# The first mixers' loop: sigmoids written as tanh, and inverse roots as a power on GpSimd ahead of the gate's product

## The chip, the cores and the metric

One core of one Trainium2 chip runs one program. The metric is the device time of one execution in microseconds, the median of several runs, together with one profiled execution whose trace is read below.

## The reference

The program computes two model blocks in a row. The change is in the first block, in the part that the reference calls `retention` and `rwkv7_time_mix`. Cut to what matters:

```python
w = -softplus(-(w0 + tanh(w_lo) @ w_up)) - 0.5
decay = exp(-exp(w))                       # = exp(-exp(-0.5) * sigmoid(...))
a = sigmoid(a0 + a_lo @ a_up)
g = sigmoid(g_lo) @ g_up
kk = k * k_k;  kk = kk / max(sqrt(sum(kk * kk)), 1e-12)
k = k * (1 + (a - 1) * k_a);   b_vec = kk * a
# ... recurrent state update over 1024 positions ...
y = (y - mean) * rsqrt(var + eps) * gn_gain       # head_norm
out_rw  = (y + bonus) * g
out_ret = silu(gate_in) * head_norm(retention(q, k, v))
```

There are 8 rwkv heads of width 64 and 4 retention heads of width 128. Everything is float32. After this part come an output projection, a mixture of 32 experts, and the second block, none of which the change touches.

## The kernel before

The sequence of 1024 positions is cut into 8 tiles of 128. The stage `mix_stage` handles one tile in one *turn* (`turn(j, u, first, last)`, with t = 2j + u from 0 to 7), and all five engines have their own written-out order of instructions for a turn; they meet at semaphores only. Nothing is scheduled by a planner: what stands in the code first runs first on its engine. The work of neighbouring tiles is interleaved: turn t does the triangular solve and the outputs of tile t, prepares the decayed keys and queries of tile t+1 (`after`), and finishes the norms of tile t-1.

The names that matter here:

- ScalarE (ACT): `squash` makes the three small feature groups `lo` (tanh, copy, sigmoid), `take_lo` copies their transposes, `sigmoid_w` and `sigmoid_a` make `sg` and `ag`, `reach_ends`, `decay_on`, `decay_back` and `decay_before` take exponentials, `root_kk`, `rw_deviation` and `ret_deviation` take square roots of tiny tiles of 8 or 4 columns. `warm_up(func)` runs `func` on one column, which only makes the engine load that function's table there (`ACT_TABLE_LOAD` in the trace).
- The solve grows in steps s = 0 to 4: `reach_back(t, s)` on TensorE (PE, L1623), `spread_z` (L816, L1352), `grow` (PE, L1609), `spread_n` (`mix_xe`, L821 on VectorE and L1357 on ScalarE), and then `half` (PE, L1641), whose start serves below as the mark of a turn.
- VectorE (DVE): `add_to_state` (L844) waits for GpSimd's `fade_state`; it stands ahead of `sum_bonus` and of `spread_n(t, 3)`. `spread` sums the squares and adds epsilon (L855, L856), `norm_divide` takes a reciprocal and multiplies (L451, L452).
- GpSimd (POOL): in a turn it makes the masked blocks `pb`, squares `kk`, masks `abrb`, scales `m` (`scale_m`, L1111, L1121), weighs the bonus (`weigh`, L1094, L1096), fades the state (`fade_state`, L1102), rotates (`rotate`), multiplies `qd_t`, multiplies the gate (`open_gate`, L1126), and then scales the normed outputs of tile t-1 (`rw_leave`, L1131 to L1137, `ret_leave`, L1142 and L1145). That last group runs over into the next turn.

VectorE's order in the middle of a turn is the one line of code that the argument leans on most:

```python
spread_z(t, 3)
if not first:
    add_to_state(t - 1)
sum_bonus(t)
...
spread_n(t, 3)
mask_k(t, 0)
```

Of the kernel before, what the change touches and what calls it, by code (L numbers as in the profile page):

```python
# [15 lines left out]
P = 128  # L16
# [438 lines left out]
class MixConsts:  # L455


    def __init__(self, nc, ctx, a):
        def sb(name, shape):
# [9 lines left out]
        self.ends = sb("ends", [P, 2])  # L469
# [8 lines left out]
            (self.incl_mid[:], a["c_incl_mid"]), (self.strict_mid[:], a["c_strict_mid"]), (self.ends[:], a["c_ends"]),  # L478
            (self.k_decay[:], a["c_ret_k"]), (self.tile_decay[:], a["c_ret_tile"]),
            (self.packed_mask[:], a["c_packed"]), (self.fold[:], a["c_fold"]),  # L480
        ]
        sb("start", [P, 40])
# [25 lines left out]
def mix_stage(nc, psum, bank, ident, a, cn, rw_feat, ret_feat, mixed, early):  # L508
# [11 lines left out]
    with Stage(nc, "mix") as st:  # L520
# [4 lines left out]
        packed_mask, fold, ends, k_decay, tile_decay = cn.packed_mask, cn.fold, cn.ends, cn.k_decay, cn.tile_decay  # L525
        NP = len(PACKED_STEPS)
# [10 lines left out]
        def heads(*names):  # L537
# [39 lines left out]
        kk_stats = st.sb("kk_stats", [P, 3, RW_HEADS])  # L577
# [24 lines left out]
                 "sums_ready sg_high_ready sg_low_ready pe_passed zeroed early_high early_low first_high first_low second_high third_high last_scaled last_spread last_squared last_meant last_root rw_last ret_last last_turned last_out").split()  # L602
# [12 lines left out]
         sums_ready, sg_high_ready, sg_low_ready, pe_passed, zeroed, early_high, early_low, first_high, first_low, second_high, third_high, last_scaled, last_spread, last_squared, last_meant, last_root, rw_last, ret_last, last_turned,  # L615
# [96 lines left out]
        def _(v):  # L712
# [12 lines left out]
            def scale_kk(j, u):  # L725

                t = 2 * j + u
                link = chain(kk_order, t, 3)
                v.wait_ge(feat_ready[u], j * 32 + 32)
                v.tensor_tensor(k_scaled[:], k_(u), k_k[:], ALU.mult).then_inc(kk_scaled, 1)  # L730
                return link

            def square_kk(t):
                v.wait_ge(kk_multiplied, t + 1)
                v.tensor_reduce(kk_stats[:, 0, :], three(b_[:], RW_HEADS), AX_X, ALU.add).then_inc(kk_squared, 1)

            def unit_kk(j, u, link):
                v.wait_ge(kk_root, 2 * j + u + 1)
                link(v.tensor_scalar(kk_stats[:, 1, :], kk_stats[:, 1, :], 1e-12, None, ALU.max))
                link(v.reciprocal(kk_stats[:, 2, :], kk_stats[:, 1, :]))  # L740

            def divide_kk(link):
                link(v.tensor_tensor(three(kk[:], RW_HEADS), three(k_scaled[:], RW_HEADS), per_row(kk_stats[:, 2, :], RW_N),
# [27 lines left out]
            def rated_b(link):  # L771
                link(v.tensor_tensor(b_[:], kk[:], ag[:], ALU.mult))

            def tildes_ba(j, u):
                v.wait_ge(exp_ready, (2 * j + u) * 3 + 3)
                v.tensor_tensor(tilde_b[u][:], b_[:], p_inv[:], ALU.mult).then_inc(tilde_ready, 1)
# [77 lines left out]
            def spread(link, of, stats, heads, width, eps, spread_ready):  # L854
                link(v.tensor_reduce(stats[:, 2, 0:heads], three(of, heads), AX_X, ALU.add))  # L855
                v.tensor_scalar(stats[:, 3, 0:heads], stats[:, 2, 0:heads], 1.0 / width, eps, ALU.mult, ALU.add)\  # L856
                    .then_inc(spread_ready, 1)

            def rw_centre(t):
# [3 lines left out]
                link = chain(rw_order, t, 4)  # L863
# [6 lines left out]
            def rw_spread_out(t, link):  # L870
                v.wait_ge(rw_squared, t + 1)
                spread(link, squares, rw_stats, RW_HEADS, RW_N, RW_GN_EPS, rw_spread)

            def rw_divide(t, link):
                v.wait_ge(rw_root, t + 1)
                norm_divide(v, link, rw_stats, RW_HEADS, RW_N, y[:], rw_normed)

            def ret_centre(t):
# [3 lines left out]
                link = chain(ret_order, t, 4)  # L882
# [4 lines left out]
            def ret_spread_out(t, link):  # L887
                v.wait_ge(ret_squared, t + 1)
                spread(link, scratch[:], ret_stats, RET_HEADS, RET_D, RET_GN_EPS, ret_spread)

            def ret_divide(t, link):
                v.wait_ge(ret_root, t + 1)
                norm_divide(v, link, ret_stats, RET_HEADS, RET_D, ry[:], ret_normed)
# [4663 lines left out]
```

## Time and profile before

| what | value |
|---|---|
| median of 3 runs | 2706.67 us (2704.95 to 2709.91) |
| the profiled execution, its own time | 2709.03 us |
| its span in the trace | 2707.3 us |
| granted TensorE clock over the span | 0.972 |
| the changed stage in the span | about 357 us to 745 us |
| one turn in the middle of the stage | 44.33 us |

The table gives whole times; the part that the change can touch is the stage from 357 to 745 us, which is about a seventh of the span. Turns 2 to 6 repeat each other to 0.1 us, so one of them can be read for all. In the timeline views a row gives the start, the duration, the engine, the line, and in brackets how long the engine was idle before it and which instruction ended that wait.

### The profile page before, as it was taken

How to read it: one execution, taken by the hardware profiler on the slowest of the kernel's cores; microseconds unless marked ns; L12 is line 12 of the kernel's file. 1: busy time of each engine (PE TensorE's matmuls, PEld its weight loads, DVE VectorE, ACT ScalarE, POOL GpSimd, SP SyncE). 2: the span in 40 equal slices, each digit the busy share in tenths (PEclk: the TensorE clock that was granted, in tenths of full speed). 3: DMA queues.
4: the chain of work that ended last, by engine and by line, in shares of the span. 5: the costliest groups of instructions: out<-in, count | busy, mean ns of one | idle time of the engine just before them, and what ended most of it. 6: DMA issues, size and time to landing. Idle time of an engine off the chain costs nothing. (4 is left out here: it accounts for less than half of the span.)

```text
span 2707.3 us, 39686 instructions
## 1 busy us (share of the span) xinstructions
PE 2517.7 (93%) x14812; PEld 2066.7 (76%) x14813; DVE 1964.9 (73%) x2667; ACT 1411.4 (52%) x2182; POOL 601.5 (22%) x554
## 2 busy tenths in 40 slices
PE   8999978888897799999996899889999999999998
PEld 7988856666676688888885888668887788888776
DVE  5532157888845799999996834778778988888586
ACT  5111157888612687877875432357744433344444
POOL 0000035666601110000001500220001334432231
PEclk9999989999998899999998999999999999999999
DMA  5555321211263799999996321000221232325866
GB/s 187 192 201 221 122 90 36 74 45 62 85 233 140 270 407 414 412 414 419 412 418 235 138 58 46 1 33 32 57 94 55 78 93 62 93 85 172 210 131 183
DMA packets 168279, 454.06 MB, mean 168 GB/s; under 512 B 15260, under 2 KB 95568, under 8 KB 154832
## 3 DMA queue, kind: packets, MB, share of 16 engines
q1 hardware_dynamic: 146048, 384.62, 38.7%
q0 software_dynamic: 16336, 46.67, 6.2%
q10 hardware_dynamic: 5760, 20.97, 1.9%
q8 instruction: 85, 1.39, 0.2%
q14 instruction: 50, 0.41, 0.1%
HBM read 373.05 MB, written 79.17 MB: 167 GB/s over the span
## 5 line engine op out<-in xcount | busy, mean ns | idle before, releaser
L135 PE MATMUL psum<-part,expert_x_high 128*128 128x512 f32 x520 | 206.8, 398 | 2.9 <-issue 1.5
L137 PE MATMUL psum<-part,expert_x_low 128*128 128x512 f32 x520 | 203.8, 392 | 0.0
L135 PE MATMUL psum<-project_w_high,high 128*128 128x448 f32 (+1 forms) x512 | 194.6, 380 | 3.5 <-DVE low L399 3.5
L136 PE MATMUL psum<-project_w_low,high 128*128 128x448 f32 (+1 forms) x512 | 193.7, 378 | 0.0
L137 PE MATMUL psum<-project_w_high,low 128*128 128x448 f32 (+1 forms) x512 | 193.5, 378 | 0.0
L130 DVE TENSOR_TENSOR expert_down_low<-expert_down,expert_down_high 128x2048 fp32r<-128x2048 f32 x62 | 139.3, 2288 | 39.0 <-ACT expert_down_high L125 39.0
L130 DVE TENSOR_TENSOR expert_gate_low<-expert_gate,part 128x2048 fp32r<-128x2048 f32 x64 | 143.8, 2288 | 7.1 <-ACT part L125 7.0
L130 DVE TENSOR_TENSOR expert_up_low<-expert_up,part 128x2048 fp32r<-128x2048 f32 x64 | 143.8, 2289 | 1.0 <-ACT part L125 1.0
L135 PE MATMUL psum<-part,ffn_w_high 128*128 128x512 f32 x352 | 138.2, 392 | 5.8 <-DVE ffn_u L4715 4.1
L136 PE MATMUL psum<-ffn_b_low,ffn_w_high 128*128 128x512 f32 x352 | 137.5, 391 | 0.0
L135 PE MATMUL psum<-down_right_high,down_left_high 128*128 128x512 f32 x308 | 121.5, 395 | 9.8 <-DVE down_right_low L130 6.2
L125 ACT ACTIVATE expert_down_high<-expert_down 128x2048 fp32r<-128x2048 f32 x62 | 115.4, 1910 | 25.5 <-ACT expert_y L2658 19.8
L125 ACT ACTIVATE part<-expert_gate 128x2048 fp32r<-128x2048 f32 x64 | 119.2, 1917 | 6.3 <-DMA h_rows<-out_xs 6.3
L137 PE MATMUL psum<-down_right_high,down_left_low 128*128 128x512 f32 x308 | 121.3, 394 | 0.0
L136 PE MATMUL psum<-down_right_low,down_left_high 128*128 128x512 f32 x308 | 121.2, 394 | 0.0
L125 ACT ACTIVATE part<-expert_up 128x2048 fp32r<-128x2048 f32 x64 | 119.1, 1916 | 0.0
L5015 POOL TENSOR_TENSOR ffn_sums<-ffn_w 128x512 f32<-128x512 f32 x19 | 38.8, 2042 | 353.1 <-DMA ffn_w<-in_ffn_w_up_dram 353.1
L2763 POOL COPY expert_pick<-ids 128x1 int32 x30 | 16.7, 556 | 447.4 <-PE psum L2566 447.4
L135 PEld LDWEIGHTS psum<-part,expert_x_high 128*128 128x128 f32 x520 | 98.2, 189 | 23.0 <-issue 1.8
L125 ACT ACTIVATE ffn_w_high<-ffn_w 128x1024 fp32r<-128x1024 f32 x44 | 44.5, 1052 | 135.2 <-POOL ffn_sums L5021 135.2
L137 PEld LDWEIGHTS psum<-part,expert_x_low 128*128 128x128 f32 x520 | 98.1, 189 | 21.2
L135 PEld LDWEIGHTS psum<-project_w_high,high 128*128 128x128 f32 x512 | 96.5, 189 | 17.9 <-DVE low L399 4.3
(780 smaller groups left out, 7471.4 us busy)
## 6 DMA issues: line engine op xcount, KB each, us to landing
expert_gate<-in_w_gate_dram SPq DMA_DIRECT2D x32, 2048.0 KB, 10.0
expert_up<-in_w_up_dram SPq DMA_DIRECT2D x32, 2048.0 KB, 9.9
expert_down<-in_w_down_dram SPq DMA_DIRECT2D x32, 2048.0 KB, 10.6
ffn_w<-in_ffn_w_up_dram SPq DMA_DIRECT2D x44, 512.0 KB, 4.6
y_rows<-expert_y ACTq DMA_DIRECT2D x32, 512.0 KB, 10.7
down_right_raw<-in_ffn_w_down_dram SPq DMA_DIRECT2D x44, 256.0 KB, 3.6
hidden_rows<-ffn_hidden SPq DMA_DIRECT2D x20, 512.0 KB, 2.8
ffn_hidden<-hidden_rows SPq DMA_DIRECT2D x20, 512.0 KB, 6.7
```

The source lines that it names most:

```text
L125: return act.activation(high, x, ACT.Copy)
L130: return v.tensor_tensor(low, x, high, ALU.subtract)
L135: pe.matmul(out, left[0], right[0], start=start, stop=False)
L136: pe.matmul(out, left[0], right[1], start=False, stop=False)
L137: return pe.matmul(out, left[1], right[0], start=False, stop=stop)
L2763: pool.tensor_copy(pick[u][:], ids[:, at]).then_inc(picked[u], 1)
L5015: pool.tensor_tensor(s1, a21, a22, ALU.add).then_inc(summed[c], 1)
```

## The change

Three things are done in the loop of the stage.

1. Every sigmoid becomes a tanh: sigmoid(x) = (1 + tanh(x/2)) / 2. The factors and the added ones move elsewhere: into the bias of the exponentials (a new constant tile `decay_bias`), into `k_a` and `ret_gain`, which are halved once, into the scale of a copy (`take_g`), into fused operations on VectorE (`rated_b`, `tildes_ba`), into a copy that is split in two (`take_lo`), and into one added ScalarE instruction in a turn (`Identity` with bias 1 on the gate).
2. The three square roots in a turn leave ScalarE, and the reciprocals and the added epsilons leave VectorE. In their place GpSimd runs, three times in a turn, a small `tensor_scalar` and a `tensor_tensor` with the operation `pow` and the exponent -0.5 (`root`).
3. On GpSimd `root_kk` stands between `scale_m` and `weigh`, and `rw_deviation` and `ret_deviation` stand ahead of `open_gate`.

The core of the diff:

```diff
             def unit_kk(j, u, link):
-                v.wait_ge(kk_root, 2 * j + u + 1)
-                link(v.tensor_scalar(kk_stats[:, 1, :], kk_stats[:, 1, :], 1e-12, None, ALU.max))
-                link(v.reciprocal(kk_stats[:, 2, :], kk_stats[:, 1, :]))
+                v.wait_ge(kk_root, 2 * (2 * j + u) + 2)
...
-            def spread(link, of, stats, heads, width, eps, spread_ready):
-                link(v.tensor_reduce(stats[:, 2, 0:heads], three(of, heads), AX_X, ALU.add))
-                v.tensor_scalar(stats[:, 3, 0:heads], stats[:, 2, 0:heads], 1.0 / width, eps, ALU.mult, ALU.add)\
-                    .then_inc(spread_ready, 1)
+            def spread(of, stats, heads, spread_ready):
+                v.tensor_reduce(stats[:, 2, 0:heads], three(of, heads), AX_X, ALU.add).then_inc(spread_ready, 1)
+
+            def divide(stats, heads, width, out, normed):
+                v.scalar_tensor_tensor(out=three(out, heads), in0=three(out, heads), scalar=float(np.sqrt(width)),
+                                       in1=per_row(stats[:, 5, 0:heads], width), op0=ALU.mult, op1=ALU.mult).then_inc(normed, 1)
...
+            def root(stats, heads, add, op, t, ready):
+                of = stats[:, 2, 0:heads]
+                pool.tensor_scalar(of, of, add, None, op).then_inc(ready, 1)
+                pool.wait_ge(ready, 2 * t + 1)
+                pool.tensor_tensor(stats[:, 5, 0:heads], of, half_down[:, 0:heads], ALU.pow).then_inc(ready, 1)
+
+            def root_kk(t):
+                pool.wait_ge(kk_squared, t + 1)
+                root(kk_stats, RW_HEADS, 1e-24, ALU.max, t, kk_root)
...
                 scale_m(t, u)
+                if not last:
+                    root_kk(t + 1)
                 weigh(t, u)
...
+                if not first:
+                    rw_deviation(t - 1)
+                    ret_deviation(t - 1)
                 open_gate(t, u)
...
             def take_lo(j, u):
                 act.wait_ge(lo_turned, 2 * j + u + 1)
-                act.activation(lo_t[:], bank[7][:, 0:256], ACT.Copy).then_inc(lo_t_ready, 1)
+                act.activation(lo_t[:, 0:P], bank[7][:, 0:P], ACT.Copy)
+                act.activation(lo_t[:, P:2 * P], bank[7][:, P:2 * P], ACT.Identity, bias=1.0).then_inc(lo_t_ready, 1)
...
-                act.activation(sg[:], p_t[:], ACT.Sigmoid).then_inc(sg_ready, 1)
+                act.activation(sg[:], p_t[:], ACT.Tanh, scale=0.5).then_inc(sg_ready, 1)
...
-                act.activation(p_t[:], bank[6][:], ACT.Exp, scale=DECAY).then_inc(exp_ready, 1)
+                act.activation(p_t[:], bank[6][:], ACT.Exp, scale=DECAY / 2, bias=decay_bias[:, 0:1]).then_inc(exp_ready, 1)
...
-                if not last:
-                    warm_up(ACT.Exp)
-                else:
+                if last:
                     early_high_of(3)
...
-                act.activation(gate[u][:], ret_in[u][:, 3 * RET_W:4 * RET_W], ACT.Sigmoid).then_inc(gate_opened, 1)
+                act.activation(gate[u][:], ret_in[u][:, 3 * RET_W:4 * RET_W], ACT.Tanh, scale=0.5).then_inc(gate_turned, 1)
                 act.wait_ge(u_made, t + 1)
                 act.activation(u_[:], bank[1][:], ACT.Copy).then_inc(u_ready, 1)
+                act.wait_ge(gate_turned, t + 1)
+                act.activation(gate[u][:], gate[u][:], ACT.Identity, bias=1.0).then_inc(gate_opened, 1)
...
-                if not first:
-                    rw_deviation(t - 1)
...
-                if not first:
-                    ret_deviation(t - 1)
                 act.wait_ge(y_made, t + 1)
+                if not first:
+                    act.wait_ge(rw_spread, t)
                 act.activation(y_fm[:], two_banks(2)[:, :, 1, :], ACT.Copy).then_inc(y_fm_ready, 1)
```

On GpSimd, in a turn in the middle of the stage, from the masks of `abrb` to the fading of the state (`mix_m` is what `scale_m` makes, `mix_q_fm` what `weigh` makes), the order before was:

```order
L1168 TENSOR_TENSOR mix_abrb<-mix_abrb,mix_strict_incl 128x4x128 x2
L1111 TENSOR_TENSOR mix_reach_on<-mix_reach 128x4
L1121 TENSOR_TENSOR mix_m<-mix_m,mix_reach_on 64x4x64 x2
L1094 TENSOR_TENSOR mix_q_fm<-mix_feat,mix_k 128x512
L1096 TENSOR_TENSOR mix_q_fm<-mix_q_fm,mix_r_k 128x512
L1102 TENSOR_TENSOR mix_state<-mix_state,mix_tile_decay 128x512
```

At the same place the changed kernel has:

```order
L1192 TENSOR_TENSOR mix_abrb<-mix_abrb,mix_strict_incl 128x4x128 x2
L1135 TENSOR_TENSOR mix_reach_on<-mix_reach 128x4
L1145 TENSOR_TENSOR mix_m<-mix_m,mix_reach_on 64x4x64 x2
L1096 TENSOR_SCALAR mix_kk_stats<-mix_kk_stats 128x8
L1098 TENSOR_TENSOR mix_kk_stats<-mix_kk_stats,mix_half_down 128x8
L1118 TENSOR_TENSOR mix_q_fm<-mix_feat,mix_k 128x512
L1120 TENSOR_TENSOR mix_q_fm<-mix_q_fm,mix_r_k 128x512
L1126 TENSOR_TENSOR mix_state<-mix_state,mix_tile_decay 128x512
```

Two small instructions now stand between `scale_m` and `weigh`, and so ahead of the fading. At the end of the turn, where the product of the gate stands, GpSimd's order in the changed kernel is this; the first and the last three rows stood next to each other before:

```order
L1202 TENSOR_TENSOR mix_qd_t<-mix_q_t,mix_q_decay 128x512
L1096 TENSOR_SCALAR mix_rw_stats<-mix_rw_stats 128x8
L1098 TENSOR_TENSOR mix_rw_stats<-mix_rw_stats,mix_half_down 128x8
L1096 TENSOR_SCALAR mix_ret_stats<-mix_ret_stats 128x4
L1098 TENSOR_TENSOR mix_ret_stats<-mix_ret_stats,mix_half_down 128x4
L1150 TENSOR_TENSOR mix_gate<-mix_gate,mix_ret_in 128x512
L1155 TENSOR_TENSOR mix_y<-mix_y,mix_rw_gain 128x512
L1158 TENSOR_TENSOR mix_y<-mix_y,mix_bonus_v 128x512
```

The gate's product, which waited for the gate alone, now also stands behind the sums of squares of both norms. On ScalarE the same stretch (from the keys of the retention, `mix_k_t`, to the next `mix_b_t`) before was:

```order
L1472 ACTIVATE mix_k_t<-psum 128x512
L1243 ACT_TABLE_LOAD
L1243 ACTIVATE mix_warm<-ident 128x1
L1475 ACTIVATE mix_q<-psum 128x512
L1270 ACTIVATE mix_y_fm<-mix_y 128x512
L1480 ACTIVATE mix_gate<-mix_ret_in 128x512
L1482 ACTIVATE mix_u<-psum 128x512
L1199 ACTIVATE mix_lo<-mix_feat 128x64
L1200 ACTIVATE mix_lo<-mix_feat 128x64
L1201 ACTIVATE mix_lo<-mix_feat 128x128
L1274 ACTIVATE mix_scratch<-mix_ry 128x512
L1262 ACT_TABLE_LOAD
```

and it now reads:

```order
L1489 ACTIVATE mix_k_t<-psum 128x512
L1491 ACTIVATE mix_q<-psum 128x512
L1290 ACTIVATE mix_y_fm<-mix_y 128x512
L1496 ACTIVATE mix_gate<-mix_ret_in 128x512
L1498 ACTIVATE mix_u<-psum 128x512
L1500 ACTIVATE mix_gate<-mix_gate 128x512
L1233 ACTIVATE mix_lo<-mix_feat 128x64
L1234 ACTIVATE mix_lo<-mix_feat 128x64
L1235 ACTIVATE mix_lo<-mix_feat 128x128
L1296 ACTIVATE mix_scratch<-mix_ry 128x512
L1511 ACTIVATE mix_y_fm<-psum 128x512
```

Both table loads are gone here, and the square of the retention's rows (`mix_scratch`) has the new gate instruction ahead of it. In the whole stage 39 table loads stood in ScalarE's order and 1 does now.

## Rows read from the trace of the kernel before

**Rows 1.** Page: busy time, share of the span, instructions, by engine.

```profile
PE 2517.7 (93%) x14812; PEld 2066.7 (76%) x14813; DVE 1964.9 (73%) x2667; ACT 1411.4 (52%) x2182; POOL 601.5 (22%) x554
```

**Rows 2.** Windows: busy us (instructions) of PE, PEld, DVE, ACT, POOL; clock.

```profile
557.00:601.30 44.30, 38.90 (x502) 28.78 (x502) 37.52 (x70) 35.90 (x79) 30.22 (x28) 1.00 0.18 60
```

**Rows 3.** Timeline of TensorE in turn 4.

```profile
571.61 0.65 PE L1623 MATMUL psum<-mix_xe,mix_pb 128*32 128x128 f32 x16 [0.20 <-ACT mix_xe L1357]
...
575.97 0.69 PE L1641 MATMUL psum<-mix_xe,mix_abrb 32*32 32x32 f32 x32 [0.31 <-issue]
...
586.79 2.00 PE L1839 MATMUL psum<-mix_q,mix_x_t 128*128 128x64 f32 x16 [0.22 <-ACT mix_q L1475]
...
592.64 0.66 PE L1712 MATMUL psum<-ident,mix_y_fm 128*128 128x128 f32 x4 [0.55 <-ACT mix_y_fm L1495]
```

**Rows 4.** Timeline of VectorE in turn 4.

```profile
565.19 0.69 DVE L735 TENSOR_REDUCE mix_kk_stats<-mix_b 128x8 f32<-128x512 f32 x1
...
569.15 0.69 DVE L844 TENSOR_TENSOR mix_state<-mix_state,psum 128x512 f32<-128x512 f32 x1 [0.62 <-POOL mix_state L1102]
...
570.47 0.88 DVE L821 COPY mix_xe<-psum 32x256 f32<-32x256 f32 x2
...
589.34 0.53 DVE L856 TENSOR_SCALAR mix_rw_stats<-mix_rw_stats 128x8 f32<-128x8 f32 x1
...
590.99 0.67 DVE L855 TENSOR_REDUCE mix_ret_stats<-mix_scratch 128x4 f32<-128x512 f32 x1
...
593.29 0.19 DVE L451 RECIPROCAL mix_rw_stats<-mix_rw_stats 128x8 f32<-128x8 f32 x1
```

**Rows 5.** Tile mix_state: who waited for GpSimd, us, times.

```profile
  DVE mix_state L844: 3.1, 5
```

**Rows 6.** Timeline of GpSimd in turns 3 to 4.

```profile
549.95 1.27 POOL L1131 TENSOR_TENSOR mix_y<-mix_y,mix_rw_gain 128x512 f32<-128x512 f32 x1 [4.44 <-DVE mix_y L452]
...
563.50 0.21 POOL L1111 TENSOR_TENSOR mix_reach_on<-mix_reach 128x4 f32<-128x4 f32 x1
563.78 1.62 POOL L1121 TENSOR_TENSOR mix_m<-mix_m,mix_reach_on 64x256 f32<-64x256 f32 x2
565.48 1.27 POOL L1094 TENSOR_TENSOR mix_q_fm<-mix_feat,mix_k 128x512 f32<-128x512 f32 x1
...
568.07 1.05 POOL L1102 TENSOR_TENSOR mix_state<-mix_state,mix_tile_decay 128x512 f32<-128x512 f32 x1
...
588.45 1.40 POOL L1126 TENSOR_TENSOR mix_gate<-mix_gate,mix_ret_in 128x512 f32<-128x512 f32 x1 [2.85 <-ACT mix_gate L1480]
594.28 1.27 POOL L1131 TENSOR_TENSOR mix_y<-mix_y,mix_rw_gain 128x512 f32<-128x512 f32 x1 [4.44 <-DVE mix_y L452]
```

**Rows 7.** Timeline of ScalarE in turn 4: start, duration.

```profile
569.31 1.28 ACT L1243 ACT_TABLE_LOAD   x1
...
570.71 0.76 ACT L1357 ACTIVATE mix_xe<-psum 32x256 f32<-32x256 f32 x2
...
575.68 1.28 ACT L1205 ACT_TABLE_LOAD   x1
...
589.81 0.62 ACT L1274 ACTIVATE mix_scratch<-mix_ry 128x512 f32<-128x512 f32 x1
590.45 1.28 ACT L1262 ACT_TABLE_LOAD   x1
```

**Rows 8.** Groups of ScalarE: busy, mean ns, idle before.

```profile
L1243 ACT ACT_TABLE_LOAD x20 | 25.7, 1283 | 0.4
...
L1253 ACT ACTIVATE mix_p_inv<-psum 128x512 f32<-128x512 f32 x8 | 4.7, 592 | 0.0
...
L3886 ACT ACTIVATE attention_p<-psum,attention_bias 128x512 f32<-128x512 f32 x8 | 5.5, 688 | 3.4 <-DVE attention_bias L3955 3.3
```

**Rows 9.** A group of VectorE of another stage: busy, mean ns.

```profile
L3649 DVE TENSOR_SCALAR mixers_decay<-mixers_decay 128x512 f32<-128x512 f32 x8 | 3.4, 428 | 0.3
```

**Rows 10.** Windows of TensorE alone, a stretch of turn 7.

```profile
697.00:708.00 11.00, 8.35 (x82) 0.54 0.00 0
```

More of the change, by code:

```diff
@@ L481, in __init__ @@
         ]
-        sb("start", [P, 40])
+        sb("start", [P, 32])
         self.loaded = nc.alloc_semaphore(name="mix_consts_loaded")
@@ L727, in scale_kk @@
                 t = 2 * j + u
-                link = chain(kk_order, t, 3)
+                link = chain(kk_order, t, 1)
                 v.wait_ge(feat_ready[u], j * 32 + 32)
@@ L734, in square_kk @@
                 v.wait_ge(kk_multiplied, t + 1)
-                v.tensor_reduce(kk_stats[:, 0, :], three(b_[:], RW_HEADS), AX_X, ALU.add).then_inc(kk_squared, 1)
+                v.tensor_reduce(kk_stats[:, 2, :], three(b_[:], RW_HEADS), AX_X, ALU.add).then_inc(kk_squared, 1)
             def unit_kk(j, u, link):
-                v.wait_ge(kk_root, 2 * j + u + 1)
-                link(v.tensor_scalar(kk_stats[:, 1, :], kk_stats[:, 1, :], 1e-12, None, ALU.max))
-                link(v.reciprocal(kk_stats[:, 2, :], kk_stats[:, 1, :]))
+                v.wait_ge(kk_root, 2 * (2 * j + u) + 2)
             def divide_kk(link):
-                link(v.tensor_tensor(three(kk[:], RW_HEADS), three(k_scaled[:], RW_HEADS), per_row(kk_stats[:, 2, :], RW_N),
+                link(v.tensor_tensor(three(kk[:], RW_HEADS), three(k_scaled[:], RW_HEADS), per_row(kk_stats[:, 5, :], RW_N),
                                      ALU.mult))
@@ L862, in rw_centre @@
                 v.wait_ge(y_copied, t + 1)
-                link = chain(rw_order, t, 4)
+                link = chain(rw_order, t, 2)
                 total_up(link, y_raw[:], rw_stats, RW_HEADS)
@@ L1038, in _ @@
             v.wait_ge(const, 16 * len(cn.loads))
+            v.tensor_scalar(k_a[:], k_a[:], 0.5, None, ALU.mult).then_inc(halved, 1)
             link = scale_kk(0, 0)
@@ L1086, in square_kk, with rw_deviation, ret_deviation @@
                 pool.tensor_tensor(b_[:], k_scaled[:], k_scaled[:], ALU.mult).then_inc(kk_multiplied, 1)
+            def root(stats, heads, add, op, t, ready):
[6 more added lines that the diff above has]
+                root(kk_stats, RW_HEADS, 1e-24, ALU.max, t, kk_root)
+            def rw_deviation(t):
+                pool.wait_ge(rw_spread, t + 1)
+                root(rw_stats, RW_HEADS, RW_N * RW_GN_EPS, ALU.add, t, rw_root)
+            def ret_deviation(t):
+                pool.wait_ge(ret_spread, t + 1)
+                root(ret_stats, RET_HEADS, RET_D * RET_GN_EPS, ALU.add, t, ret_root)
             def weigh(t, u):
@@ L1239, in reach_ends @@
                     act.wait_ge(reach_ordered, t - 1)
-                act.activation(reach[u][:], spans[:], ACT.Exp, scale=DECAY).then_inc(reach_ready, 1)
-            def warm_up(func):
-                act.activation(warm[:], ident[:, 0:1], func)
+                act.activation(reach[u][:], spans[:], ACT.Exp, scale=DECAY / 2, bias=decay_bias[:, 3:4]).then_inc(reach_ready, 1)
             def decay_on(j, u):
@@ L1273, in square_ret @@
                 act.wait_ge(ret_centred, t + 1)
+                if is_late(t):
+                    act.wait_ge(ret_spread, t)
                 act.activation(scratch[:], ry[:], ACT.Square).then_inc(ret_squared, 1)
@@ L1433, in turn @@
                 take_t(t, 3)
-                if not last:
-                    warm_up(ACT.Exp)
-                else:
+                if last:
                     early_high_of(3)
@@ L1453, in turn @@
                     reach_ends(t + 1, 1 - u)
-                    root_kk(t + 1)
                 else:
@@ L1502, in _ @@
             take_lo(0, 0)
-            root_kk(0)
             for to, of in ((incl_high, incl_mid), (strict_high, strict_mid)):
```

68 lines of the change are left out of this document (34 added, 34 removed).

## The prediction, made before the changed kernel was run

> **What bounds the kernel now.** The page comes first: over the whole span TensorE is busy for 93%, and GpSimd for 22% [rows 1]. That average hides the changed stage, so I read it by turns. In one turn of 44.33 us TensorE is busy for 38.9, VectorE for 37.5, ScalarE for 35.9 and GpSimd for 30.2 us [rows 2]: no engine is full, and a turn is as long as a chain that passes between all of them. GpSimd, which looks free on the page, is at 68% here.
>
> Next I ask the timelines where that chain runs. I follow turn 4, and take the start of the half step on TensorE, 575.97, as its mark [rows 3]. Going back from it, VectorE works without a gap worth the name from 569.15, when it adds to the retention state. That addition waited 0.62 us for GpSimd [rows 4], and it did so in 5 turns, 3.1 us together [rows 5]: turns 2 to 6. GpSimd in turn had no pause since 549.95, when it began `rw_leave` of the turn before; that began when VectorE had divided the norms, after 4.44 us of idleness [rows 6]. So there is a loop: end of the norms on VectorE, 19.17 us of GpSimd up to the end of the fading (568.07 + 1.05 = 569.12), the addition on VectorE, the rest of the turn, and the end of the norms again. A second chain runs beside it, through ScalarE: the load of the exponential's table at 569.31 makes it copy `xe` only at 570.71, 0.24 us after VectorE began its half at 570.47 [rows 4, 7], and TensorE waited for ScalarE's half there [rows 3]. The two chains are equal within about 0.1 us. Shortening one alone gives little.
>
> **ScalarE, what is removed.** 38 of the stage's 39 table loads go, 1.28 us each [rows 8], 49 us of its time. What each was worth is read from who waited behind it:
> - Before `spread_n(t, 3)`: GpSimd's chain takes over at once. In turns 0 and 1 that chain does not bind, and 0.35 us are gained.
> - Before the copy of `q`: TensorE waited 0.22 us for it [rows 3]; worth 0.22 in every turn.
> - Before the two square roots (590.45 [rows 7]): TensorE waits 0.55 us for the copy of `y_fm` behind them [rows 3]. Worth 0.55, with the 0.22 above some 0.77, at the start of the next turn.
> - The load at 575.68 [rows 7], and the one at the head of a turn, run while ScalarE would wait for TensorE anyway: nothing.
>
> The Trainium skill (ScalarE: Activation LUTs, "What ACT_TABLE_LOAD costs") puts a switch at 1283 ns plus about 1380 ns of drain; by that, 38 switches would be an estimated 101 us of ScalarE. Here the load is 1283 ns, but the activation behind it starts at once; the order shows the one point on which trace and page agree, that tanh and exp need no switch between them.
>
> **ScalarE, what is added.** The gate's `Identity` costs about 0.6 us, the time from one 128x512 activation to the next. The split of `take_lo` costs about 0.17, on the path of `spread_n(t, 0)`, where both engines finish together. A bias from a tile costs 0.10 (0.688 against 0.592 [rows 8]); three of these stand where ScalarE is now ahead, at nothing. Without that lead they would cost 0.3 in a turn.
>
> **VectorE.** At the end of a turn it works without a pause and bounds the end of the norms. The epsilon of the rwkv norm (589.34, 0.45 to the next start), that of the retention norm (about 0.1), and the reciprocal (593.29, 0.22 to the next start) go [rows 4]. But the retention's reduction at 590.99 waits for ScalarE's square, which sits at 589.81 [rows 7]: with the 0.22 gained and the 0.6 of the gate added it can end no earlier than about 590.8, so of the 0.45 only some 0.15 remains there; the division then ends 0.6 to 0.65 earlier. The second reciprocal, at the head of the next turn, gives 0.2. Together with the 0.77, capped by what VectorE reaches, the masked product that starts the solve comes 0.95 earlier; less 0.17 for `take_lo`, the solve of every turn from 2 runs 0.8 us ahead, **if** GpSimd allows it. The two small instructions on `kk_stats` lie in slack before a wait for TensorE: nothing. The fused forms last as long as those that they replace.
>
> **GpSimd, what is added.** Call p the duration of the power on 128x8. No row shows one. The lower bound is the smallest product, 0.21 on 128x4, with 0.28 from its start to the next one's [rows 6]. Above, the nearest row is a full 128x512 product, 1.27 [rows 6]; nothing in the trace excludes more, since a power is other arithmetic. From these two a multiplication costs (1.27 - 0.21) / 512, about 2 ns per column; if a power costs some twenty of those, 8 columns add 0.33. I choose **p = 0.5**, nearer to the small row, since most of a tiny instruction is fixed. One root is then 0.28 + p + 0.08 = 0.36 + p, that is 0.86 us, three times in a turn. The skill (GPSIMD Engine Reference, section 3.1) puts data-dependent branching at about 12 cycles per element; that would be an estimated 0.1 us for 8 columns, so p about 0.3 and the sum by it 1 us lower. No row here can show it.
>
> - `root_kk` stands ahead of `weigh` and the fading. `kk_squared` came at 565.87 (565.19 + 0.69 [rows 4]), GpSimd came to the place at 565.48, so the two are about level. With the solve 0.8 ahead the fading ends at 565.87 - 0.8 + 0.08 + 0.36 + p + 3.64 (from 565.48 to 569.12 [rows 6]), which is 569.15 + p: **later** by 0.03 + p.
> - The roots ahead of the gate: GpSimd waits for `ret_spread`, about 591.5. Then 0.08 + 0.36 + p + 1.40 for the gate, + 0.08: `rw_leave` starts at 593.4 + p, against 594.28 before [rows 6], 0.88 - p earlier. By VectorE it could be 0.65 earlier. At p = 0.5 it is 0.38 earlier, and the fading 0.36 + p - 0.38 = 0.48 later, about the same as the 0.53 by the first path. The gate's product was finished 4.4 us early; that cover is now spent. Queued behind it are `rw_leave` and `ret_leave`, and the `pb` masks of the next turn, for which nobody waits yet. The loads of the next retention input wait for the gate as well, and have a whole turn of slack.
>
> So in each of turns 2 to 6 VectorE waits for GpSimd longer than before, about 2 us in place of 0.62, and the mark of the turn moves by 0.53 - 0.1 (a gap before `mask_k` closes) = **+0.43 us**.
>
> **The sum.** Prologue: the halving of `k_a` adds 0.43 [rows 9] and the first root about 0.15 more than the two steps that it replaces; the load before the exponentials gives 0.45 back and a wait for the sigmoid 0.2: -0.1. Turns 0 and 1: -0.35 - 0.22 + 0.17 = -0.4 each. Turns 2 to 6: 5 x 0.43 = +2.15. Turn 7 has no `root_kk`, so its solve keeps the 0.95: -0.9; in its tail one table load stands before a square root that VectorE needs later: 0. Total -0.1 - 0.8 + 2.15 - 0.9 = +0.35. On the profiled execution: 2709.03 + 0.35 = 2709.4; it lay 2.4 above the median, so a median of **2707**.
>
> **The rivals.**
> - *GpSimd takes over, p from 0.2 to 0.95* (the forecast). At p = 0.2 a turn costs +0.13, in all -1; from about 0.6 the gate's path rules, a turn costs 2p - 0.62, at 0.9 +1.18, in all +5: 2706 to 2712. For it speaks that the wait for the fading is there already. Chance 0.61.
> - *The power is dear* (the other side). The loop of GpSimd holds two roots, so a turn costs 2p - 0.62. From p = 1 the whole is above +5.4. At 1.5 it is 5 x 2.4 - 1 = +11, 2718; at 3 about +28, 2735. For it: power is the one operation of which no row exists, and it stands twice in the tightest loop. Against it: only 8 columns. Chance 0.25.
> - *The lead of the solve comes through* (faster). If GpSimd's block of 19.17 us shrinks by over 1 us, for instance because products like the gate's, 1.40 beside a busy VectorE, fall to the 1.27 of the others [rows 6], all seven turns gain about 0.8 to 0.9: -0.8 - 7 x 0.8 = -6.4, 2700. Against it: the same instructions still overlap. Chance 0.10.
> - *The clock moves.* In turn 7 the granted clock was 0.54 (the 1.2 GHz level) over 11 us [rows 10], after TensorE had stood in waits of 1 us; matmuls took 1.08 in place of 0.65, and the turn some 2 us more. Longer waits of TensorE could bring this into other turns, an earlier turn 7 could lose it: -2 or +3 to +9. Chance 0.04 beside the others.
> - That the loads remain is excluded by the order.
>
> **How the numbers follow.** About 0.2%, 5.4 us, is what a measurement can tell here from no change. Faster: the third rival and a share of the clock, 0.11. Slower: the second and the rest of the clock, 0.27. Within: 0.62. The range of 8 in 10 takes the third rival's 2700 and the second one's up to p about 1.4, 2716; the likeliest case alone has 2705 to 2712.
>
> **What would show it.** In the changed trace: one table load in the stage; ScalarE's busy time down by about 45 us; the rows of the power give p at once; VectorE's wait at the state's addition in turns 2 to 6 near 2 us (at 0.6 or none, the third rival); the turn near 44.8 us in place of 44.33; the gate's product within 0.1 us of the start of `rw_leave`; the wait of TensorE for `y_fm` gone. The prediction is wrong if p is above 1, if GpSimd's other instructions change their length, or if the clock falls in more turns.

## The result and the profile after

The changed kernel took 2748.66 us, median of 4 runs (2745.46 to 2749.48), against 2708.29 us for the kernel before in the same session (4 runs, 2704.95 to 2715.33). The ratio is 1.0142, 95% interval 1.0129 to 1.0156: slower by 1.4%, where 2707 us, range 2700 to 2716, was predicted. The profiled execution took 2748.18 us, its span is 2745.7 us and its mean clock 0.960. Of the runs below, one of the ten of `mult_for_pow` ran at a clock of 0.902 (2760.08 us) and is left out of its row.

First the page's busy line, which answers to [rows 1]:

```profile
PE 2542.4 (93%) x14812; PEld 2088.4 (76%) x14813; DVE 1948.6 (71%) x2624; ACT 1364.1 (50%) x2116; POOL 642.3 (23%) x600
```

ScalarE is relieved by 47.3 us (about 45 were predicted), and the span is 38.4 us longer. GpSimd has 40.8 us more work, TensorE 24.7 us more with the same number of matmuls. The next view groups the new instructions on GpSimd (busy us, mean ns, idle before):

```profile
L1098 POOL TENSOR_TENSOR mix_kk_stats<-mix_kk_stats,mix_half_down 128x8 f32<-128x8 f32 x8 | 13.3, 1668 | 0.7
L1098 POOL TENSOR_TENSOR mix_rw_stats<-mix_rw_stats,mix_half_down 128x8 f32<-128x8 f32 x7 | 13.3, 1898 | 0.6
L1098 POOL TENSOR_TENSOR mix_ret_stats<-mix_ret_stats,mix_half_down 128x4 f32<-128x4 f32 x7 | 7.5, 1065 | 0.6
```

So p is 1.67 us (1.90 for the rwkv norm), and 1.07 us with 4 columns. The prediction took 0.5. The tile of the state shows who pays, to be read beside [rows 5]:

```profile
  DVE mix_state L846: 17.1, 7
```

The wait of VectorE for the fading went from 3.1 to 17.1 us, and from 5 turns to 7. In turn 4, to be read beside [rows 4] (the first row is the sum of squares of the retention's norm, the second that of the keys):

```profile
563.88 0.69 DVE L857 TENSOR_REDUCE mix_ret_stats<-mix_scratch 128x4 f32<-128x512 f32 x1
...
584.21 0.69 DVE L738 TENSOR_REDUCE mix_kk_stats<-mix_b 128x8 f32<-128x512 f32 x1
...
590.68 0.69 DVE L846 TENSOR_TENSOR mix_state<-mix_state,psum 128x512 f32<-128x512 f32 x1 [2.52 <-POOL mix_state L1126]
```

The turn's marks (start of the half step on TensorE) were 400.21, 442.81, 487.16, 531.64, 575.97, 620.31, 664.66 and 711.10 us before, and are now 402.87, 448.28, 498.27, 548.10, 598.20, 648.37, 698.11 and 744.57. The first mark is 2.7 us later; the step into turn 1 costs 2.8 us, the five to turn 6 between 5.4 and 5.8 each, the last one nothing, and 4.9 us come behind the last mark. Together that is the 38.4. The steps repeat from turn to turn; the first and the last of these figures are differences of one trace each, and the section on the prediction says how far they carry.

GpSimd in the same place of a turn as [rows 6]:

```profile
562.71 0.62 POOL L1096 TENSOR_SCALAR mix_rw_stats<-mix_rw_stats 128x8 f32<-128x8 f32 x1 [4.17 <-DVE mix_rw_stats L857]
563.42 1.93 POOL L1098 TENSOR_TENSOR mix_rw_stats<-mix_rw_stats,mix_half_down 128x8 f32<-128x8 f32 x1
565.43 0.23 POOL L1096 TENSOR_SCALAR mix_ret_stats<-mix_ret_stats 128x4 f32<-128x4 f32 x1
565.75 1.02 POOL L1098 TENSOR_TENSOR mix_ret_stats<-mix_ret_stats,mix_half_down 128x4 f32<-128x4 f32 x1
566.75 1.27 POOL L1150 TENSOR_TENSOR mix_gate<-mix_gate,mix_ret_in 128x512 f32<-128x512 f32 x1
567.97 1.72 POOL L1155 TENSOR_TENSOR mix_y<-mix_y,mix_rw_gain 128x512 f32<-128x512 f32 x1
...
575.31 2.77 POOL L1186 TENSOR_TENSOR mix_pb<-mix_pk,mix_packed_mask 128x256 f32<-128x256 f32 x4
...
585.06 0.25 POOL L1096 TENSOR_SCALAR mix_kk_stats<-mix_kk_stats 128x8 f32<-128x8 f32 x1 [1.42 <-DVE mix_kk_stats L738]
585.39 1.67 POOL L1098 TENSOR_TENSOR mix_kk_stats<-mix_kk_stats,mix_half_down 128x8 f32<-128x8 f32 x1
587.02 1.28 POOL L1118 TENSOR_TENSOR mix_q_fm<-mix_feat,mix_k 128x512 f32<-128x512 f32 x1
...
589.61 1.04 POOL L1126 TENSOR_TENSOR mix_state<-mix_state,mix_tile_decay 128x512 f32<-128x512 f32 x1
```

The two roots of the norms stand in front of the gate's product for 4.04 us (562.71 to 566.75), and `rw_leave` starts right behind it. From there to the end of the fading it is 22.68 us, against 19.17 before: the root of the keys takes 1.96 (585.06 to 587.02), and GpSimd waits 1.42 for the sum of their squares. What TensorE does meanwhile (the answer to [rows 3]):

```profile
576.29 0.65 PE L1638 MATMUL psum<-mix_xe,mix_pb 128*32 128x128 f32 x16 [1.73 <-POOL mix_pb L1186]
576.86 0.44 PE L1647 MATMUL psum<-ident,mix_nf 128*128 128x128 f32 x2
577.23 1.97 PE L1546 MATMUL psum<-mix_lora_up,mix_lo_t 64*128 64x512 f32 x2
579.13 1.08 PE L1624 MATMUL psum<-mix_ze,mix_tf 128*32 128x128 f32 x16
580.14 2.08 PE L1756 MATMUL psum<-mix_ret_in,mix_rot 128*128 128x128 f32 x8
...
592.98 0.64 PE L1638 MATMUL psum<-mix_xe,mix_pb 128*32 128x128 f32 x16 [1.94 <-DVE mix_xe L823]
...
595.18 1.08 PE L1624 MATMUL psum<-mix_ze,mix_tf 128*32 128x128 f32 x16 [0.20 <-DVE mix_ze L818]
596.19 2.08 PE L1590 MATMUL psum<-mix_ar_t,mix_kt_t 64*128 64x256 f32 x8
598.20 1.06 PE L1656 MATMUL psum<-mix_xe,mix_abrb 32*32 32x32 f32 x32
```

Two waits are new: 1.73 us for the `pb` masks, now late behind `rw_leave` and `ret_leave`, and 1.94 us for `xe` (0.20 before), behind VectorE's wait at the state. Behind each, the same matmuls last longer: the half step 1.06 us in place of 0.69 [rows 3]. The windows of these stretches (busy us and count of each engine, then the clock) say why:

```profile
570.00:576.00 6.00, 4.11 (x51) 2.68 (x49) 4.43 (x7) 5.13 (x13) 5.84 (x6) 1.00 0.01 1
577.00:583.00 6.00, 6.00 (x44) 3.44 (x44) 2.98 (x6) 3.40 (x8) 5.87 (x7) 0.53 0.00 0
583.00:592.00 9.00, 6.39 (x79) 4.20 (x72) 4.53 (x10) 5.50 (x14) 7.31 (x8) 0.93 0.35 126
593.00:599.00 6.00, 5.80 (x80) 4.35 (x82) 4.22 (x6) 4.25 (x11) 5.61 (x5) 0.62 0.20 51
```

The granted clock falls towards its 1.2 GHz level behind each of the two waits (0.53 over 6 us behind the first, 0.62 over 6 us behind the second). Before the change it was 1.00 over a whole turn [rows 2].

### The profile page after: what moved, and what is told of

The parts are those of the page before. It is cut to its first block and busy times, and to the rows that moved or that the text cites. A ratio compares the mean times of both kernels' runs of the same rounds, so it can differ in the third digit from the quotient of the medians.

```text
span 2745.7 us, 39637 instructions
## 1 busy us (share of the span) xinstructions
PE 2542.4 (93%) x14812; PEld 2088.4 (76%) x14813; DVE 1948.6 (71%) x2624; ACT 1364.1 (50%) x2116; POOL 642.3 (23%) x600
## 5 line engine op out<-in xcount | busy, mean ns | idle before, releaser
L125 ACT ACTIVATE ffn_w_high<-ffn_w 128x1024 fp32r<-128x1024 f32 x44 | 44.4, 1052 | 135.3 <-POOL ffn_sums L5037 135.3
```

Source lines behind the costliest of these rows:

```text
L125: return act.activation(high, x, ACT.Copy)
```

## The experiments

The theory after the trace: all of the loss is the power's duration on GpSimd, by way of two late results and of a clock that falls behind them. The rivals: the tanh side costs something; the order on GpSimd and not the power is at fault; the slow clock only goes along with the waits and costs nothing. In all tables "turn" is the median of the five distances between the marks from turn 1 to turn 6, "clock" the mean of 470 to 670 us, "wait" VectorE's wait at the state's addition over the stage. These three are read from one profiled execution each. It lies within about 3 us of the kernel's median, except for `mult_for_pow` (2706.34, 6 below) and `masks_first` (2727.89, 7 above). Where an expectation speaks of the kernel before, its median beside these runs was 2708.3 to 2711.1 us.

**1. The two halves of the change apart.** `tanh_alone` has the tanh forms and keeps the roots on ScalarE and the reciprocals on VectorE, with 29 of the 39 table loads; `roots_alone` keeps the sigmoids and their tables. One line of many from each, against the changed kernel:

```diff
 # tanh_alone
-                    root_kk(t + 1)              # GpSimd
+                act.activation(kk_stats[:, 4, :], kk_stats[:, 2, :], ACT.Sqrt).then_inc(kk_root, 1)
 # roots_alone
-                act.activation(sg[:], p_t[:], ACT.Tanh, scale=0.5).then_inc(sg_ready, 1)
+                act.activation(sg[:], p_t[:], ACT.Sigmoid).then_inc(sg_ready, 1)
```

> The sigmoids from tanh as in the change, but the roots as before: square roots on ScalarE, reciprocals on VectorE, nothing added on GpSimd but one product ahead of the loop. Table loads in a turn: 4 in place of 5; the one ahead of spread_n(t, 3) goes. By my sum the load's gain is capped by GpSimd's chain, and the gate's added instruction and the split copy cost: 2704 to 2714, no change that can be measured. Rival: the removed load and the rest give 0.3 us and more in a turn, below 2703; or the tanh edits are a cost of their own, above 2715.

> The roots on GpSimd as in the change, but the sigmoids as before with their tables (2 loads in a turn are left, exponential and sigmoid). Theory A: the roots carry the whole loss: 2738 to 2758. If tanh and roots each carry a part, it lies between 2712 and 2735.

**2. A cheap operation in the power's place.** In `mult_for_pow` the operation is a multiplication by 0.0005 (the value that `half_down` then holds), so the norms are wrong and the experts are chosen otherwise; the instructions of this stage and their places stay. The later stages get other data, so the two kernels of this group are compared by their turns first:

```diff
-                pool.tensor_tensor(stats[:, 5, 0:heads], of, half_down[:, 0:heads], ALU.pow).then_inc(ready, 1)
+                pool.tensor_tensor(stats[:, 5, 0:heads], of, half_down[:, 0:heads], ALU.mult).then_inc(ready, 1)
```

> One operation differs: the power with exponent -0.5 is a multiplication by 0.0005 on the same tiles, so the norms come out wrong and the experts are chosen differently; the time is read from the turns of the changed stage, which take 50.1 us from half step to half step in the changed kernel and 44.33 in the one before. Theory A (the power's 1.67 us on 8 columns and 1.02 on 4, in GpSimd's loop, set off everything, the clock included): the small products fall to about 0.25 us and the turn to 44.0 to 45.0. Rival C (the order itself, the waits and the edits for tanh cost, whatever the operation): the turn stays above 47.

`same_length` adds spare products to it, to learn whether the power harms by more than its time:

```diff
+                for n in range(5 if stats is kk_stats else 3):
+                    pool.tensor_tensor(spare[:, n, 0:heads], of, half_down[:, 0:heads], ALU.mult).then_inc(spared, 1)
```

> mult_for_pow (multiplication in the place of the power, so the norms are wrong) with spare products of the same small tile ahead of each, 5 for the keys' root and 3 for each of the others, so that a root lasts about as long as with the power: some 1.6 us, 1.2 to 1.9 and 1.1 us. If only the time on GpSimd matters, a turn is back at about 50 us and the whole at 2740 to 2750. If the power does harm in another way as well (a lock of the shared memory, a slower neighbour), the whole stays below 2730.

| kernel | median us (range, runs) | ratio, 95% | turn | clock | wait |
|---|---|---|---|---|---|
| before | 2708.29 (2704.95 to 2715.33, 4) | | 44.4 | 1.00 | 3.1 |
| changed | 2748.66 (2745.46 to 2749.48, 4) | 1.0142, 1.0129 to 1.0156 | 50.0 | 0.88 | 17.1 |
| roots_alone | 2741.93 (2740.41 to 2744.75, 4) | 1.0122, 1.0105 to 1.0140 | 50.3 | 0.90 | 18.6 |
| tanh_alone | 2712.11 (2704.96 to 2718.00, 10) | 1.0001, 0.9987 to 1.0016 | 44.4 | 1.00 | 3.1 |
| mult_for_pow | 2712.80 (2706.34 to 2718.70, 9) | 1.0015, 1.0003 to 1.0027 | 44.7 | 0.98 | 10.1 |
| same_length | 2731.27 (2725.27 to 2737.35, 6) | 1.0080, 1.0062 to 1.0097 | 47.9 | 0.94 | 15.5 |

The roots alone bring 1.22 of the 1.42% (and the same turn, 50.3 against 50.0); the tanh forms alone change nothing that can be measured. The rest, some 6 us, appears only where both are present; no run shows what it is, and the intervals overlap. With a multiplication in the same places a turn is 44.7 us. So the order, with all the rest of the change, costs 0.4 us in a turn, and the power the other 5.3. (One of these five turns took 46.5 us; see the clock below.)

`same_length` reached neither of its two cases, 2740 to 2750 or below 2730, because its premise failed. Products that don't wait for each other start about 0.16 us apart on GpSimd:

```profile
555.78 0.61 POOL L1101 TENSOR_SCALAR mix_rw_stats<-mix_rw_stats 128x8 f32<-128x8 f32 x1 [4.17 <-DVE mix_rw_stats L858]
556.47 0.81 POOL L1104 TENSOR_TENSOR mix_spare<-mix_rw_stats,mix_half_down 128x8 f32<-128x8 f32 x3
557.24 0.20 POOL L1106 TENSOR_TENSOR mix_rw_stats<-mix_rw_stats,mix_half_down 128x8 f32<-128x8 f32 x1
```

So the roots took 4.15 us in a turn (2.86 and 1.29), not the 6.00 of the power (4.04 and 1.96); the multiplication alone has 2.88. (All are stretches of GpSimd's time; where the roots are short, they include its wait for the second sum, 0.28 us in `same_length` and 0.77 in `mult_for_pow`.) Against 2.88, 4.15 and 6.00 us of roots a turn has 44.7, 47.9 and 50.0: 2.5 us of turn for each us at first and 1.1 then. The time that GpSimd is held explains it, and nothing calls for a harm of the power beside it; that is argued from three points, not shown apart.

**3. What a power costs.** `power_sizes` runs eight of them ahead of the stage:

```diff
+            for n, (parts, cols) in enumerate(((P, 1), (P, 2), (P, 4), (P, 8), (P, 16), (P, 64), (32, 8), (32, 64))):
+                pool.tensor_tensor(ry[0:parts, n * 64:n * 64 + cols], scratch[0:parts, 0:cols], ry_raw[0:parts, 0:cols], ALU.pow)\
+                    .then_inc(sized, 1)
```

> The changed kernel with eight powers more on GpSimd ahead of the stage, of 1, 2, 4, 8, 16 and 64 columns on 128 partitions and of 8 and 64 columns on 32 partitions, base 2 and exponent -0.5. If the power's cost is by the column, about 0.16 us each beside 0.4 fixed: 0.55, 0.7, 1.0, 1.7, 3.0 and 10.7 us. If it is a fixed start and a cheap stream: all below 3 us. If partitions share its units, 32 partitions cost less than 128; if each lane has its own, the same.

Its groups on GpSimd, each shape apart (the whole took 2766.57 us, one run; the stage's first mark is 24.4 us later than in the changed kernel):

```profile
L1222 POOL TENSOR_TENSOR mix_ry<-mix_scratch,mix_ry_raw 128x64 f32<-128x64 f32 x1 | 10.5, 10537 | 0.0
L1222 POOL TENSOR_TENSOR mix_ry<-mix_scratch,mix_ry_raw 32x64 f32<-32x64 f32 x1 | 10.5, 10536 | 0.0
L1222 POOL TENSOR_TENSOR mix_ry<-mix_scratch,mix_ry_raw 128x16 f32<-128x16 f32 x1 | 2.9, 2890 | 0.0
L1222 POOL TENSOR_TENSOR mix_ry<-mix_scratch,mix_ry_raw 128x8 f32<-128x8 f32 x1 | 1.6, 1627 | 0.0
...
L1222 POOL TENSOR_TENSOR mix_ry<-mix_scratch,mix_ry_raw 128x4 f32<-128x4 f32 x1 | 1.0, 1002 | 0.0
...
L1222 POOL TENSOR_TENSOR mix_ry<-mix_scratch,mix_ry_raw 128x1 f32<-128x1 f32 x1 | 0.6, 583 | 0.1
```

From 1 to 64 columns it is (10537 - 583) / 63 = 158 ns a column, on top of some 0.42 us, the same for 32 and for 128 partitions. A plain product took about 2 ns a column: the power is some 76 products, not twenty. All eight have the base 2 and the exponent -0.5; with the stage's own data 8 columns took 1.67 us, against 1.63 here.

**4. Where the roots stand.** `kk_behind` moves the keys' root, `gate_first` the two others, `both_moved` all three:

```diff
 # kk_behind
-                if not last:
-                    root_kk(t + 1)
                 weigh(t, u)
                 if not first:
                     fade_state(t - 1)
+                if not last:
+                    root_kk(t + 1)
 # gate_first
-                if not first:
-                    rw_deviation(t - 1)
-                    ret_deviation(t - 1)
                 open_gate(t, u)
+                if not first:
+                    rw_deviation(t - 1)
+                    ret_deviation(t - 1)
```

> root_kk stands behind the fading of the state instead of ahead of weigh. Theory A: the wait of VectorE at the state's addition (2.5 us in the changed kernel) goes to below 0.6, since 1.42 us of waiting for the sum of squares and 1.96 of the root leave the path; the turn falls from 50.1 to 46.5 to 48.0, in total 12 to 22 us less. If the roots at the end of the turn and the late masks of pb alone set the turn, it stays above 49.

> The two roots of the norms stand behind the gate's product instead of ahead of it. If the gate's product in that place is the costly part, rw_leave starts 1.3 us earlier and the turn is 1 to 2 us shorter, 8 to 12 us in total. My own reckoning: the roots still end at the same time, since GpSimd has to do the product and 3.6 us of roots between the end of the first sum of squares and rw_leave, so VectorE's division now waits about 0.6 us for the root, and the turn stays within 0.5 us of 50.1, the total within 5 us.

> root_kk behind the fading and the two roots of the norms behind the gate's product. The single moves gave -27 and -2 us. If the first had hidden the second's effect, the two together give clearly more, below 2715. My reckoning from the first two traces: the second move only shifts 1.3 us of product against 3.6 us of roots, the total is that of the first move alone within 5 us, 2717 to 2727.

`masks_first` is `kk_behind` with the late masks taken out of the way:

```diff
+                if t > 1:
+                    ret_leave(t - 2, u)         # behind the pb masks of the turn
...
                 if last:
                     scale_gates(u)
-                if not first:
                     ret_leave(t - 1, 1 - u)     # here in the last turn alone
```

> Beside root_kk behind the fading, ret_leave of a tile stands behind the masks of pb of the next turn instead of ahead of them, so that the masks come 2.9 us earlier. In the run with root_kk behind the fading TensorE waited 1.7 us for these masks in each turn and then ran at its lower clock for a while. Theory: both go, the turn falls from about 46.2 to 43.5 to 44.5, the total to 2702 to 2712. If the wait for the masks only stood in for another wait as long, the total stays at 2718 to 2725.

| kernel | median us (range, runs) | ratio, 95% | turn | clock | wait |
|---|---|---|---|---|---|
| gate_first | 2747.04 (2740.85 to 2751.38, 4) | 1.0128, 1.0100 to 1.0155 | 51.2 | 0.91 | 19.5 |
| kk_behind | 2721.98 (2718.57 to 2727.34, 7) | 1.0045, 1.0029 to 1.0061 | 45.8 | 0.92 | 1.2 |
| masks_first | 2720.85 (2714.39 to 2732.36, 7) | 1.0036, 1.0014 to 1.0057 | 46.9 | 0.93 | 16.7 |
| both_moved | 2719.55 (2717.39 to 2720.66, 5) | 1.0037, 1.0022 to 1.0051 | 45.1 | 0.98 | 4.5 |

Moving one root by three instructions takes two thirds of the loss away (26.7 of 40.4 us, more than the 12 to 22 expected); moving the two others does nothing that can be told apart. The timelines of GpSimd and VectorE in `gate_first` show why:

```profile
616.32 1.44 POOL L1150 TENSOR_TENSOR mix_gate<-mix_gate,mix_ret_in 128x512 f32<-128x512 f32 x1 [4.01 <-ACT mix_gate L1500]
617.85 0.57 POOL L1096 TENSOR_SCALAR mix_rw_stats<-mix_rw_stats 128x8 f32<-128x8 f32 x1
```

```profile
615.35 0.68 DVE L857 TENSOR_REDUCE mix_rw_stats<-mix_y_fm 128x8 f32<-128x512 f32 x1
```

The gate comes from ScalarE (the added `Identity`, L1500) about when the sum of squares comes from VectorE, which ended at 616.03 (615.35 + 0.68). The root now stands behind the gate's product and starts 1.8 us after its sum, which uses up the 1.3 us that this product no longer takes behind the roots. In `kk_behind` the wait at the state is gone, but TensorE still waits for the masks, in the timeline of its turn 4:

```profile
564.66 0.64 PE L1638 MATMUL psum<-mix_xe,mix_pb 128*32 128x128 f32 x16 [1.74 <-POOL mix_pb L1186]
...
570.87 1.08 PE L1638 MATMUL psum<-mix_xe,mix_pb 128*32 128x128 f32 x16
```

`masks_first` missed its expectation. That wait did go, and another came back; its timeline, first VectorE, then TensorE:

```profile
579.32 0.69 DVE L846 TENSOR_TENSOR mix_state<-mix_state,psum 128x512 f32<-128x512 f32 x1 [3.34 <-POOL mix_state L1126]
```

```profile
581.62 0.82 PE L1639 MATMUL psum<-mix_xe,mix_pb 128*32 128x128 f32 x16 [2.93 <-DVE mix_xe L823]
```

The moved `ret_leave` now lies between the masks and the fading. With the power on GpSimd its order decides who waits and for how long, and none of these four orders brings a turn back to 44.4: the best turn, in `both_moved`, is 45.1.

**5. The clock.** `keep_warm` fills the two waits of the changed kernel with matmuls whose result nobody reads; `warm_late` does so from turn 2 on, and `moved_warm` does the same on `both_moved`. The fence has the form of `warm_late`:

```diff
             def reach_back(t, s):
+                if t > 1 and s in (1, 4):                     # keep_warm: without t > 1
+                    for _ in range(12 if s == 1 else 14):
+                        pe.matmul(bank[1][:, 0:P], ident[:], ident[:], start=True, stop=True)
                 wait_n(t, s)
```

> The changed kernel with 12 and 14 idle matmuls of 128x128 on TensorE ahead of the waits of the steps 1 and 4 of the solve, in a bank that nobody reads; nothing else moves. Theory B (a large share of the 5.8 us per turn is TensorE at its lower clock level after those waits): the granted clock in the turns rises from 0.86 to about 1.0, the turn falls from 50.1 to 46 to 47.5, the total by 15 to 25 us. Theory A in its pure form (GpSimd's instructions alone set the turn, the slow stretches lie beside them): the turn stays within 1 us of 50.1.

> The changed kernel with the idle matmuls of keep_warm, but only in turns 2 to 7, since in turns 0 and 1 there was no wait to fill and they cost some 4 us there. If the clock's share of the loss is 2.3 us in a turn as keep_warm showed: turns 0 and 1 as in the changed kernel, the later ones about 47.8, and the whole at about 2738 us, 10 below the changed kernel. If the lower level of the clock costs nothing by itself: 2748 or above.

> both_moved (the keys' root behind the fading, the two others behind the gate's product) with the idle matmuls in turns 2 to 7. If what is left of the loss there is the clock (its turns were 45.1 and one 47.8 us): turns of 45.1 throughout and 2716 us. If the idle matmuls now stand in the path, since the waits that they fill are gone: turns of 46 us or more and 2724 or above. The kernel before is beaten in neither case.

| kernel | median us (range, runs) | ratio, 95% | turn | clock | wait |
|---|---|---|---|---|---|
| keep_warm | 2742.62 (2740.89 to 2744.09, 4) | 1.0116, 1.0094 to 1.0137 | 47.7 | 1.00 | 18.1 |
| warm_late | 2738.64 (2734.61 to 2741.72, 5) | 1.0103, 1.0086 to 1.0120 | 47.9 | 1.00 | 18.6 |
| moved_warm | 2739.87 (2734.84 to 2745.91, 6) | 1.0114, 1.0097 to 1.0130 | 49.4 | 1.00 | 0 |

The windows view of 470 to 670 us, in the changed kernel and then in `warm_late` (the clock is the third number from the end):

```profile
470.00:670.00 200.00, 174.00 (x2018) 130.66 (x2017) 140.48 (x253) 119.94 (x280) 144.09 (x133) 0.88 0.16 53
```

```profile
470.00:670.00 200.00, 185.70 (x2301) 145.54 (x2302) 146.06 (x265) 123.97 (x290) 151.88 (x140) 1.00 0.16 53
```

In `keep_warm` the fill is two rows in a turn, and the matmuls behind them have their old length:

```profile
577.05 2.94 PE L1635 MATMUL psum<-ident 128*128 128x128 f32 x24
...
582.07 0.64 PE L1624 MATMUL psum<-mix_ze,mix_tf 128*32 128x128 f32 x16
...
592.01 3.39 PE L1635 MATMUL psum<-ident 128*128 128x128 f32 x28
```

More work on TensorE makes a turn 2.1 us shorter (47.9 for 50.0; `keep_warm` 2.3), though VectorE waits as long as before. So at least 2.1 of the 5.6 us that a turn lost are the lower clock; at least, because the 6.3 us of filling are more than the 3.7 us of waits that they fill. `keep_warm` as a whole is only 6 us below the changed kernel, where 15 to 25 were expected, and its turn of 47.7 lies between the two cases of its expectation; its first mark is 4.9 us later (407.81, where other traces scatter by 3 us) and the step to turn 1 is 2.4 us longer, since there was no such wait to fill. `warm_late`, which leaves these turns alone, is 10 us below, as expected.

The lower clock also holds up GpSimd: in `warm_late` it waits 0.64 us for the keys' sum of squares, in place of 1.42:

```profile
582.85 0.24 POOL L1096 TENSOR_SCALAR mix_kk_stats<-mix_kk_stats 128x8 f32<-128x8 f32 x1 [0.64 <-DVE mix_kk_stats L738]
```

On `both_moved` the same filling has no wait long enough to hide in: its turn grows by 4.3 us, the second case of its expectation. The length of a wait does not settle the clock by itself: in `mult_for_pow` the clock stayed at 1.00 behind a wait of 0.84 us at 559.07, and one turn later, behind a wait of the same length, it was 0.51 (the windows are 559 to 566 and 604 to 611 us):

```profile
559.00:566.00 7.00, 5.97 (x82) 4.07 (x86) 5.48 (x10) 5.72 (x14) 6.84 (x9) 1.00 0.28 80
604.00:611.00 7.00, 7.00 (x60) 4.03 (x52) 3.71 (x7) 4.02 (x10) 6.25 (x9) 0.51 0.01 2
```

That turn took 46.5 us in place of 44.7; `both_moved` has one such turn of 47.8. Why this turn and not its neighbours, no run shows. None of the twelve kernels beats the kernel before.

## Why the prediction was wrong

**The step that failed** is the size of one term, p, the duration of the power: "I choose p = 0.5, nearer to the small row, since most of a tiny instruction is fixed". The same paragraph said that nothing excluded more, and the row that it was nearest to was another kind of arithmetic. A power is 1.67 us on 8 columns and 1.07 on 4. Its own rival, "the power is dear", held the right mechanism: with p = 1.67 its 2p - 0.62 gives 2.7 us in a turn and 2709.0 + 5 x 2.7 - 1 = 2721.6 us in all. (The 1 is a slip: the sum of the prediction has 0.1 + 0.8 + 0.9 = 1.8 in that place, which makes it 2720.8; and for p = 3 the same formula gives +26, not +28.) The loop holds three roots in the trace and not two, since the next root starts only at 565.43, behind the rwkv norm's, while the retention's sum is there at 564.57 (563.88 + 0.69); the third, of 4 columns, is short enough (1.32 us) that the end of the gate's product comes where two roots of 1.67 put it.

The profiled time was 2748.2, another 27 us. The five turns lost 28.0 us where the rival's formula gives 13.6. What was priced at nothing or nearly so:

- The `pb` masks, "for which nobody waits yet". At p = 0.5 that held; with 4 us of roots ahead of `rw_leave` TensorE waits 1.73 us for them. A slack that had not been measured was left out of the rival.
- "The clock moves", chance 0.04 "beside the others". It was no case of its own but a consequence of the second rival: the dear power made TensorE wait 1.73 and 1.94 us in a turn, and the lower level behind these waits took 2.1 us or more per turn, some 10 us or more over five turns. By bounds alone the rival's price should have risen faster than 2p.
- The five turns became six (2.8 us more in turn 1), since with these roots GpSimd's chain binds there too.
- Ahead of the stage's first mark 0.15 us was priced for the first root. VectorE's product with it starts at 365.57 in place of 363.96, so it cost 1.6. The mark itself is 2.7 later, but one trace does not settle the rest: in four kernels that are the same up to there (`kk_behind`, `masks_first`, `both_moved`, `moved_warm`) it lies between 401.19 and 404.73.
- Behind the last mark, where 0 was said, there are 4.9 us more (2001.1 against 1996.2). They cannot be put down to the change: `roots_alone`, with the same power, has 1994.0 there, and `tanh_alone`, without it, 1999.5. Where they come from stays open.

**What held.** ScalarE's busy time fell by 47.3 us (45 predicted), with one table load left in the stage; `y_fm`'s wait is gone; tanh and exp need no switch; two chains of equal length meant that relief of ScalarE alone brings nothing, which `tanh_alone` bears out for the loads that it removes (10 of the 39; ratio 1.0001). With p near 0.2, `mult_for_pow` gives +0.4 us in a turn where +0.13 was worked out, and its median of 2712.8 lies inside the predicted range, 0.8 above the likeliest case. One sign came true by luck: VectorE's wait at the addition was forecast at about 2 us and is 2.5 in turn 4, though the turn grew by 5.6 and not by 0.43. That wait shows that GpSimd binds, not by how much.

The Trainium skill (GPSIMD Engine Reference, section 3.1) puts data-dependent branching at about 12 cycles per element, from which an estimated p of 0.3 was worked out. The measured 158 ns per column are far above that estimate, and the measurement decides. For the table loads, the prediction called the missing switch between tanh and exp the one point on which trace and page agree; the 1283 ns of a load are another.

## What to carry to other kernels

An operation that no row of the trace shows must not be priced by its shape: put it once into an idle stretch and read its row (here eight rows settled it) before giving it a place in the tightest loop. When a term can make TensorE wait in a new place, price the clock together with that term, not as a separate chance. And an engine that is busy for two thirds of a turn, in a chain that binds, is not idle: a dear instruction goes behind the result that others wait for, which here was worth 27 of 40 us. Here it was best not moved at all (`tanh_alone`, ratio 1.0001, against 1.0036 to 1.0045 for the three orders with the keys' root behind the fading).

## What the runs showed of the hardware

- A power on GpSimd costs 158 ns per column over some 0.42 us, for 32 as for 128 partitions: 0.58 us for 1 column, 10.54 for 64. A full product of 512 columns takes 1.27 us.
- Small products that don't wait for each other start about 0.16 us apart on GpSimd and are listed at 0.20 us each, so their durations overlap and must not be added up.
- Two waits of TensorE of 1.73 and 1.94 us in a turn of 50 us were each followed by matmuls at the 1.2 GHz level (0.53 over the 6 us behind the first). Where matmuls without a use filled these waits, the granted clock stayed at 1.00 and a turn became 2.1 us shorter. A wait of 0.84 us was followed by the lower level in one turn of `mult_for_pow` (0.51 over 7 us) and by none in the turn before it.
